# Expert weight loads of a two-block network: one DMA queue against two

## The reference

```python
def hierarchical_moe(h, w_router_group, w_router_expert, w_gate, w_up, w_down):
    t = h.reshape(-1, d)
    ...
    expert_id = g_sel[:, None] * EXPERTS_PER_GROUP + top_local
    ...
    def expert_block(args):
        xb, e = args
        hid = jax.nn.silu(xb @ w_gate[e]) * (xb @ w_up[e])
        return hid @ w_down[e]
```

## Time and profile before

| | us |
|---|---|
| median of 3 runs | 1657.46 |
| lowest and highest | 1656.88, 1661.55 |
| the profiled execution | 1659.11 |
| its span | 1657.3 |
| TensorE busy | 1506.3 (91%) |
| VectorE, ScalarE busy | 574.6, 452.0 |
| bytes moved | 489.21 MB |

### The profile page before, as it was taken

One profiled execution on the slowest core, in us unless ns is written; L12 is line 12 of the kernel. 1 busy time (PEld: TensorE's weight loads), 2 busy tenths in 40 slices (PEclk: granted clock), 3 DMA queues, 4 the chain that ended last, 5 costly groups with the idle time before them and its releaser, 6 DMA issues.

```text
span 1657.3 us, 20152 instructions
## 1 busy us (share of the span) xinstructions
PE 1506.3 (91%) x7956; PEld 944.9 (57%) x7958; DVE 574.6 (35%) x926; ACT 452.0 (27%) x720; POOL 27.7 (2%) x36
## 2 busy tenths in 40 slices
PE   7999978999979987879999898889889889999996
PEld 5897868988759977763343343434334333444342
DVE  5745656654464897631111011111101101111112
ACT  5435645533444554421111011111101111111111
POOL 1000000000000000120000000000000000000000
PEclk9999989999989997979999999999999999999998
DMA  8563343455334332577999999999999999999993
GB/s 295 167 235 109 120 152 135 173 203 183 122 116 139 103 102 72 194 300 332 422 406 429 429 428 428 429 429 428 429 429 427 429 429 384 408 425 415 418 397 138
DMA packets 80269, 489.21 MB, mean 295 GB/s; under 512 B 6423, under 2 KB 8595, under 8 KB 56788
## 3 DMA queue, kind: packets, MB, share of 16 engines
q1 hardware_dynamic: 79028, 484.17, 72.4%
q0 software_dynamic: 1184, 4.26, 0.8%
HBM read 506.20 MB, written 1.08 MB: 306 GB/s over the span
## 4 chain that ended last, share of the span: by engine, by line
PE 61%; DMA 15%; DVE 8%; issue 2%; ACT 1%; SPq 1%; DVEq 0%; ACTq 0%
PE bank L1156 23%; PE bank L818 20%; DMA slots<-in_w_up_dram 15%; PE bank L1192 8%; PE bank L1126 4%; PE bank L1136 2%; DVE w_split L1292 1%; DVE h_lo L1282 1%; DVE areas L1542 1%; DVE xeT L1726 1%; PE bank L801 1%; SPq L394 1%; PE bank L1075 1%; PE bank L1104 0%; PE bank L1065 0%
## 5 line engine op out<-in xcount | busy, mean ns | idle before, releaser
L1156 PE MATMUL bank<-slots,xeT 128*64 128x512 f32 x1536 | 356.4, 620 | 48.0 <-DMA slots<-in_w_up_dram 47.9
L1156 PEld LDWEIGHTS bank<-slots,xeT 128*64 128x64 f32 x1536 | 118.9, 143 | 280.4 <-issue 280.4
L1292 DVE TENSOR_TENSOR w_split<-raw,w_split 128x2048 fp32r<-128x2048 f32 (+2 forms) x98 | 209.1, 2168 | 75.4 <-ACT w_split L543 75.4
L1192 PE MATMUL bank<-slots,heT 128*64 128x512 f32 x1024 | 226.8, 595 | 7.5 <-ACT heT L747 7.5
L818 PE MATMUL bank<-w_split,h_hi 128*128 128x512 f32 (+1 forms) x688 | 213.8, 393 | 8.4 <-DVE h_lo L1282 3.3
L818 PE MATMUL bank<-h_hi,w_split 128*128 128x256 f32 x1120 | 206.9, 285 | 0.3 <-DVE h_lo L1282 0.3
L543 ACT ACTIVATE w_split<-raw 128x2048 fp32r<-128x2048 f32 (+2 forms) x98 | 173.6, 1817 | 62.3 <-PE bank L818 56.7
L818 PEld LDWEIGHTS bank<-h_hi,w_split 128*128 128x128 f32 x1120 | 176.7, 193 | 2.2 <-issue 0.8
L1735 DVE TENSOR_TENSOR h_e<-bank,h_e 128x512 f32<-128x512 f32 x32 | 22.1, 692 | 433.2 <-PE bank L1156 433.2
L818 PE MATMUL bank<-h_lo,w_split 128*128 128x256 f32 x560 | 159.0, 284 | 0.0
L1192 PEld LDWEIGHTS bank<-slots,heT 128*64 128x64 f32 x1024 | 70.7, 137 | 144.9 <-issue 133.5
(11 more groups left out here) (295 smaller groups left out, 1390.5 us busy)
## 6 DMA issues: line engine op xcount, KB each, us to landing
slots<-in_w_up_dram SPq DMA_DIRECT2D x64, 2048.0 KB, 18.9
slots<-in_w_down_dram SPq DMA_DIRECT2D x64, 2048.0 KB, 15.2
areas<-in_w_gate_dram SPq DMA_DIRECT2D x32, 2048.0 KB, 14.2
slots<-in_w_gate_dram SPq DMA_DIRECT2D x32, 2048.0 KB, 21.3
raw<-in_w_in_dram SPq DMA_DIRECT2D x42, 1024.0 KB, 6.1
raw<-in_w_ff_dram SPq DMA_DIRECT2D x32, 1024.0 KB, 5.2
raw<-in_w_out_dram SPq DMA_DIRECT2D x12, 1024.0 KB, 5.0
raw<-in_w_ple_gate_dram SPq DMA_DIRECT2D x4, 1024.0 KB, 5.6
```

The lines of the kernel that those rows point to most:

```text
L1156: last = mm(bank[SLOTS * e:SLOTS * e + SLOTS, :], xeT[:, k, odd, SLOTS * e:SLOTS * e + SLOTS], expert_panel(w, e, odd)[:, k, :], start=(k ...
L1192: last = mm(banks[half][SLOTS * e:SLOTS * e + SLOTS, :], heT[:, c, SLOTS * e:SLOTS * e + SLOTS], expert_panel("down", e, odd)[:, c, 512 * ...
L1292: last = tt(lo, source, hi, ALU.subtract)
```

## The change

SyncE's `load` gets a parameter `both`. In `rest_of_pass` it is false, so there SyncE issues only the first expert's panel of each pair. The second expert's panel is issued by ScalarE, with a new function `load_second`: it reads the token count into a register and issues the DMA on ScalarE's own queue. The gate panel of pair i+2 is issued after the SiLU of pair i, the up panel of pair i+1 after `gates_seen` (and, in odd pairs, after the second copy of gathered tokens), the down panel of pair i+1 after `y_hi`. The panels of the first pair, and the gate panels of the second, are still issued by SyncE alone. How many pairs ahead a panel is loaded stays as it was on both queues: gate two, up and down one.

```diff
-            def load(w, i, pair, odd, beyond):
+            def load(w, i, pair, odd, beyond, both=True):
...
-                for e in range(2):
+                for e in range(2 if both else 1):
...
-                            load(w, 2 * j + n + ahead + first, 2 * j + n + ahead, (n + ahead) % 2, beyond)
+                            load(w, 2 * j + n + ahead + first, 2 * j + n + ahead, (n + ahead) % 2, beyond, both=False)
                 for w in ("up", "down"):
-                    load(w, first + PAIRS - 1, PAIRS - 1, 1, beyond)
+                    load(w, first + PAIRS - 1, PAIRS - 1, 1, beyond, both=False)
...
+            def load_second(w, pair, odd, beyond):
+
+                weights = {"gate": w_gate, "up": w_up, "down": w_down}[w]
+                tokens = act.value_load(count_i[0:1, bass.ds(2 * pair + 1, 1)], min_val=0, max_val=S)
+                act.dma_start(expert_panel(w, 1, odd), weights[0, 2 * pair + 1].rearrange("(p k) n -> p k n", p=P),
+                              cond=tokens > beyond).then_inc(pair_landed["odd_gate" if w == "gate" and odd else w, 1], 16)
+
-            def experts(couple, odd, first=False, last=False):
+            def experts(couple, odd, in_pass, beyond, first=False, last=False):
...
                 act_(h_e[:, :], banks[2][:, :], ACT.Silu).then_inc(silu_ready, 1)
+                if not last:
+                    load_second("gate", 2 * in_pass + odd + 2, odd, beyond)
...
                 if odd and not last:
                     gather(couple + 1, 1)
+                if not (odd and last):
+                    load_second("up", 2 * in_pass + odd + 1, 1 - odd, beyond)
...
                     act_(y_hi[:, 512 * half:512 * half + 512], banks[half][:, :], ACT.Copy, scale=gate_of_slot).then_inc(ye_a, 1)
+                if not (odd and last):
+                    load_second("down", 2 * in_pass + odd + 1, 1 - odd, beyond)
...
+            act.wait_ge(marks_done, 1)
+            experts(0, 0, 0, 0, first=True)
+            experts(0, 1, 0, 0)
-            experts(0, 0, first=True)
-            experts(0, 1)
-            act.wait_ge(marks_done, 1)
```

More of the change, by code:

```diff
@@ L757, in experts @@
                     act_(y_hi[:, 512 * half:512 * half + 512], banks[half][:, :], ACT.Copy, scale=gate_of_slot).then_inc(ye_a, 1)
+                if not (odd and last):
+                    load_second("down", 2 * in_pass + odd + 1, 1 - odd, beyond)
             gather(0, 0)
             gather(0, 1, 2)
-            experts(0, 0, first=True)
-            experts(0, 1)
             act.wait_ge(marks_done, 1)
+            experts(0, 0, 0, 0, first=True)
+            experts(0, 1, 0, 0)
             fullest = act.value_load(count_i[0:1, NE:NE + 1], min_val=0, max_val=S)
             with act.Fori(1, PAIRS // 2 - 1) as j:
[L766 to L769, removed]
+                experts(j, 0, j, 0)
+                experts(j, 1, j, 0)
+            experts(PAIRS // 2 - 1, 0, PAIRS // 2 - 1, 0, last=True)
+            experts(PAIRS // 2 - 1, 1, PAIRS // 2 - 1, 0, last=True)
             with act.If(fullest > SLOTS):
@@ L774, in _ @@
                     with act.Fori(0, PAIRS // 2 - 1) as j:
[L775 to L778, removed]
+                        experts(r * (PAIRS // 2) + j, 0, j, r * SLOTS)
+                        experts(r * (PAIRS // 2) + j, 1, j, r * SLOTS)
+                    experts(r * (PAIRS // 2) + (PAIRS // 2 - 1), 0, PAIRS // 2 - 1, r * SLOTS, last=True)
+                    experts(r * (PAIRS // 2) + (PAIRS // 2 - 1), 1, PAIRS // 2 - 1, r * SLOTS, last=True)
             load_roots()
```

## The result

The median is 1668.01 us (four runs, 1663.50 to 1669.06) against 1657.17 us before: a ratio of 1.0054, with a 95% interval of 1.0029 to 1.0080. The medians are 10.8 and 5.3 us apart, and the two intervals overlap from 1.0029 to 1.0048: the change makes the kernel slower by some 5 to 8 us. The forecast was 1660 us, 2.4 us above the time before.

What follows compares the result with a forecast made beforehand. The prediction took the DMA engines to bound the mixture from 862 to 1353 us. Issue work and lateness added 0 us, panel order 4 x 0.6 = +2.4 us: 1657.46 + 2.4, rounded to 1660 us, range 1650 to 1676.

Steps and rivals of the forecast that it cites:

- What bounds it: Mixture, 862 to 1353 us: DMA engines never rest, 7.0 us per couple too slow for TensorE; savings elsewhere vanish there.
- The faster rival: Long stretch and after: two queues keep engines fuller, 434 instead of 428 GB/s, 7.7 us faster, 1650 us; chance 0.14.
- ScalarE and SyncE worth nothing: SyncE's saved issues gain nothing; ScalarE's count reads and issues, about 1.2 us each, hide under waits of 5 us or more.
- The lateness of the up panel covered: Odd pairs: second up panel issued 4.8 us behind the first, under 6.6 us of cover; costs 0 us.
- The order among the queues, +2.4 us: Where the queue runs dry, SyncE's later panels delay the awaited one: 0.6 us at each of four places.
- the first wait: TensorE's first wait for an up panel, one of the four places taken to lose 0.6 us each.
- the waits behind the skipped loads: Three or four waits after loads skipped for experts without tokens, where the queue can run dry; 0.6 us each.
- The term's upper bound: Panel order between queues: the whole up-panel lateness of 4.1 us lost at each of four places, 16 us.
- The likeliest case: Whole kernel: the time lies within 5 us of the forecast of 1660 us; chance 0.48.
- the slower cases: One queue ahead for good, 1672.5 us, or ScalarE's issue over 1.8 us later than reckoned, 1663 to 1665; together 0.38.
- the slower rival: Odd pairs' up-panel wait: a lasting lead above 3.9 us empties queues, 15 us lost, 1672.5; chance within the joint 0.38.
- the 0 us that the prediction worked out from the rule: Panel order between queues: engines taking turns of some 9 to 17 descriptors would keep the old order, 0 instead of +2.4 us.

Runs made afterwards that it cites:

- run 9: Changed kernel with both queues only in couples 3 to 9, SyncE alone issuing before and after: 1658.93 us, ratio 1.0004 to the kernel before.
- run 4: Changed kernel, but only the second down panels go through ScalarE, gate and up staying with SyncE: 1681.51 us, ratio 1.0132 to the kernel before.
- run 3: Kernel before, one queue, with the second up panel of each pair made to wait for `gates_seen`: 1657.96 us, ratio 0.9995.
- run 2: Changed kernel with ScalarE issuing the second up panel as soon as `upped` allows: 1663.62 us, ratio 1.0031 to the kernel before.
- the four traces with the full loss: Traces of the changed kernel, its unedited repeat, its early-up-panel version (1663.62 us), and its version with two queues only in couples 0 to 2 and 10 to 15 (1664.97 us).
- the larger comparison: Changed kernel measured again without edit, 12 runs, against the kernel before: 1664.5 us against 1659.23, ratio 1.0036 (1.0024 to 1.0048).
- runs 5 and 6: Changed kernel with only the second gate panels, then only the second up panels, through ScalarE: 1658.68 us, ratio 0.9999, and 1659.08 us, ratio 1.0006.
- run 6: Changed kernel with only the second up panels through ScalarE's queue: 1659.08 us, ratio 1.0006 to the kernel before.

## Why the prediction was right and wrong

**What bounds it: right.** The mixture is held by the DMA engines from 862 to 1353 us. The two queues of the change neither raise nor lower their rate (428 GB/s), couples stay 58.8 us apart (up products at 1061.71 and 1120.48), and what the change does there vanishes: shown by the stretches and by run 9. It is no rule for every split: run 4 does lose there. The faster rival (434 GB/s) is refuted.

**ScalarE and SyncE worth nothing: right.** No wait of TensorE for ScalarE was added on the path (7.5 us for `heT`, before and after), and an issue with its count read came to the 1.2 us reckoned or less.

**The lateness of the up panel covered: right.** 4.7 us measured; run 3 shows that 3.5 us cost nothing with one queue, and run 2 that taking the lateness away wins next to nothing.

**The order among the queues, +2.4 us: the step that failed, by its size.** The mechanism was named, with the first wait and the waits behind the skipped loads as its places. The size, 0.6 us at each of four places, had no row behind it. The runs show 33 to 44 packets of lead at such a place, 1.3 to 1.7 us at 428 GB/s (an estimate). The waits of pairs 1, 5 and 25 are 1.1 to 2.1 us longer than before in the four traces with the full loss; that of pair 29 is longer in one of them only (4.7 us against 3.2). Three things were missed. First, the lead of SyncE's queue does not come from the late issue, as the step had it: run 2 takes the lateness away and keeps the loss. How a queue starts up while the other is busy (below) may be its source. Second, the places: pair 1, which had no wait before, has one now, while the first wait of before, pair 5, stands at the head of the long stretch, which pays its loss back. Third, a longer wait can also bring the slower clock. The prediction saw that behaviour in the earlier trace rows and did not put it into this term. It is certain only at pair 5 (9.7 to 9.9 us for the product in all four traces with the full loss), where it is paid back; the 1.7 us at pair 25 are in one trace of the four. What the clock adds to the loss of the medians stays open. Measured, the term is 5.3 us in the larger comparison, with an interval of 4 to 8, and 10.8 us between the medians of the smaller one, instead of 2.4 us. The term's upper bound was 16 us, and the time stayed inside the range; but a range of 26 us around an expected 2.4 us would have held most outcomes, and says little for the sum.

**The likeliest case was the wrong one.** "Within 5 us" had 0.48 and the slower cases 0.38; both comparisons come out slower by more than 0.3%, though both intervals reach under it (1.0029 and 1.0024). The 1668 us of the first lie 8 us above the forecast; the 5.3 us of the second would still lie within its 5 us. But the slower rival as written, a lead that never goes away and opens gaps in the long stretch, did not happen: the share there stayed at 1.01. The lead did stay, 34 packets at pair 5 and still 18 at pair 21, but that is 1.3 us and less, under the 3.9 us that the rival asked for. Gaps did open in run 4, where only down panels jump the line, with 0.99, 419 GB/s and 67.4 us of waits. That the change escapes this because the second panels of all three kinds move together is argued, not shown. So the chances were split by the right question, and the forecast itself was priced too low.

**Left open.** That a queue's slow start is the cause of the lead is argued from the trace and from the places of the loss. No run changed it by itself, and it can't be enough alone: in runs 5 and 6 ScalarE's panels start late nearly every time, and nothing is lost.

## What to carry to other kernels

Where one queue keeps the DMA engines full, its written order is the schedule: a second queue does not add bandwidth, it can let transfers needed later overtake the one that is awaited. For this change the price appears only where the queue is shallow, at the start and behind skipped work; a worse split (run 4) pays in the saturated stretch too. The waits' total hardly shows it; compare the ends of the same product in both chains, in more than one trace. To shorten a wait for a large transfer, keep one queue and let the consumer start on its first half; here that won about 3 us, 0.2%.

## What the runs showed of the hardware

**Two queues share the engines in pieces much smaller than a panel.** From 758.4 to 762 us, with a gate panel on each queue, the changed kernel's queues moved (packets, MB, share of the 16 engines):

```profile
q1 hardware_dynamic: 48, 0.79, 50.9%
q10 hardware_dynamic: 48, 0.79, 50.9%
```

That is 3 packets of 16 KB per engine from each queue, on the average, in the same 3.6 us. The Trainium skill, "DMA: Bandwidth & Descriptors", section "Queues, rings and completion order", had turns of typically 9 to 17 descriptors. The run differs: a panel of 8 such packets per engine does not go in one piece, and the 0 us that the prediction worked out from the rule did not come.

**A queue starts slowly beside a busy one.** Just before, SyncE had issued its panel at 753.89 and ScalarE its own at 754.71 us. From 754.7 to 758.4 us the packets were these, and below them is ScalarE's panel with its time to landing:

```profile
q1 hardware_dynamic: 78, 1.28, 99.2%
...
areas<-in_w_gate_dram ACTq DMA_DIRECT2D x1, 2048.0 KB, 13.5
```

No packet of q10 is among them: ScalarE's transfer moved nothing for 3.7 us after its issue, while SyncE's, issued with both queues idle, had moved its first packets about a microsecond after its own. On one queue the second gate panel landed 11.7 us after its issue:

```profile
areas<-in_w_gate_dram SPq DMA_DIRECT2D x1, 2048.0 KB, 11.7
```

So SyncE's queue wins a lead of some five packets per engine here, 3 us. The same lag stands in the other direction and in the saturated stretch. SyncE's up panel issued at 785.53 us, when its queue had run empty, moved nothing up to 788.9 us, while ScalarE's queue did. In run 6, ScalarE's up panel issued at 867.64 us moved nothing up to 871 us. The changed kernel from 785.6 to 788.9 us, then run 6 from 867.7 to 871:

```profile
q10 hardware_dynamic: 83, 1.36, 97.3%
...
q1 hardware_dynamic: 86, 1.39, 98.4%
```

Not every restart is so slow: SyncE's down panel issued at 1619.87 us moved its first packet 1.1 us later, with ScalarE's queue busy. In the saturated stretch of the changed kernel both queues move packets in every microsecond, so there no queue starts anew.
